# Modulation sums of a two-block transformer kernel: column quarters of the array, a ScalarE copy and a transpose in place of matmuls with one moving column

## The reference

```
ml = ada_mods(c, ada_w[i], ada_b[i])          # six vectors of 1024 from c:  c @ ada_w[i] + ada_b[i], c through silu
mc = ada_mods(c_ctx, ada_w[i], ada_b[i])      # the same for the context, where it is still needed
hl = modulate(rms_norm_2(x, norm1_g[i]), ml[0], ml[1])
x  = x + ml[2] * yl
x  = x + ml[5] * sq_relu_mlp(modulate(rms_norm_2(x, norm2_g[i]), ml[3], ml[4]), mlp_w1[i], mlp_w2[i])
```

## Time and profile before

| what | value |
|---|---|
| median of 3 runs | 3950.78 us (3943.45 to 3952.15) |
| span of the profiled execution | 3942.7 us |
| profiled execution's own time | not listed apart from the span; the nearest of the three runs took 3943.45 us |
| TensorE busy (matmuls) | 3801.9 us, 96% of the span |
| TensorE weight loads (beside matmuls) | 2605.5 us, 66% |
| VectorE, ScalarE, GpSimd busy | 50%, 24%, 15% |
| DMA | 87 GB/s on the mean |
| granted TensorE clock, mean | 0.981 of full |

### The profile page before, as it was taken

The page is one execution under the profiler, slowest core; times in us unless marked ns, Lnnn a source line. Parts: engine busy times, 40 slices in busy tenths (PEclk is TensorE's granted clock), DMA queues, the critical chain, the costliest instruction groups (busy, mean ns, idle before and its releaser), DMA issues.

```text
span 3942.7 us, 42262 instructions
## 1 busy us (share of the span) xinstructions
PE 3801.9 (96%) x16296; PEld 2605.5 (66%) x16296; DVE 1982.2 (50%) x3455; ACT 956.5 (24%) x2193; POOL 585.3 (15%) x476
## 2 busy tenths in 40 slices
PE   9999999999999999999999899999999999999997
PEld 4458446545655566555554578888568888778886
DVE  2654345635673566555300845654765566244343
ACT  1142214621452212112201632021312111212020
POOL 1001000001000111111200511112432111111111
PEclk8999999999999999999999999999999999999999
DMA  3112331022002123323112414443202444112221
GB/s 130 64 44 87 99 106 56 1 76 86 25 1 63 65 90 124 120 94 128 54 64 76 80 44 150 171 167 101 75 22 86 170 172 150 70 64 86 86 86 43
DMA packets 226949, 342.46 MB, mean 87 GB/s; under 512 B 32256, under 2 KB 100512, under 8 KB 226720
## 3 DMA queue, kind: packets, MB, share of 16 engines
q1 hardware_dynamic: 201552, 321.65, 23.8%
q0 software_dynamic: 6816, 10.01, 1.3%
q10 hardware_dynamic: 18384, 8.11, 0.8%
HBM read 334.08 MB, written 4.06 MB: 86 GB/s over the span
## 4 chain that ended last, share of the span: by engine, by line
PE 90%; DVE 4%; ACT 2%; issue 1%; POOL 1%; DMA 0%; ACTq 0%; DVEq 0%; POOLq 0%
PE psum L1743 44%; PE psum L1493 30%; PE psum L1861 3%; PE psum L1808 3%; PE psum L1838 2%; PE psum L1599 1%; PE psum L1453 1%; DVE small L2735 1%; ACT arena L2192 1%; POOL arena L2916 1%; PE psum L1551 1%; PE psum L1522 1%; PE psum L1534 1%; ACT arena L2180 0%; PE psum L1820 0%
## 5 line engine op out<-in xcount | busy, mean ns | idle before, releaser
L1493 PE MATMUL psum<-HC,ring 128*128 128x256 f32 (+1 forms) x3152 | 1023.7, 484 | 14.2 <-ACT HC L2111 4.5
L1493 PEld LDWEIGHTS psum<-HC,ring 128*128 128x128 f32 x3152 | 599.2, 192 | 430.3 <-issue 371.6
L1743 PE MATMUL psum<-arena,ring 128*128 128x256 f32 (+1 forms) x2304 | 600.4, 416 | 5.2 <-ACT arena L1975 5.2
L1743 PEld LDWEIGHTS psum<-arena,ring 128*128 128x128 f32 x2304 | 435.5, 190 | 147.6 <-ACT arena L1975 10.0
L1743 PE MATMUL psum<-arena 128*128 128x256 f32 (+1 forms) x1792 | 472.3, 417 | 0.4
L1743 PE MATMUL psum<-HC,ring 128*128 128x256 f32 (+1 forms) x1792 | 438.5, 399 | 10.9 <-ACT arena L1975 4.7
L1743 PEld LDWEIGHTS psum<-arena 128*128 128x128 f32 x1792 | 340.4, 190 | 115.4 <-ACT arena L1980 0.7
L1743 PEld LDWEIGHTS psum<-HC,ring 128*128 128x128 f32 x1792 | 341.6, 192 | 86.7 <-issue 10.9
L2873 POOL TENSOR_TENSOR ring<-ring 128x1024 f32<-128x1024 f32 (+1 forms) x80 | 217.4, 2717 | 1220.8 <-DVE arena L2260 1199.4
L2425 DVE SCALAR_TENSOR_TENSOR arena<-ring,cond,arena 128x512 f32<-128x512 f32 x448 | 319.6, 750 | 8.0
L2329 DVE TENSOR_TENSOR arena<-psum,arena 128x384 f32<-128x384 f32 (+2 forms) x80 | 44.5, 556 | 382.6 <-PE psum L1743 382.6
(11 more groups left out here) (229 smaller groups left out, 3907.6 us busy)
## 6 DMA issues: line engine op xcount, KB each, us to landing
ring<-in_mlp_w SPq DMA_DIRECT2D x64, 2048.0 KB, 8.9
ring<-in_ada_w SPq DMA_DIRECT2D x48, 2048.0 KB, 7.9
ring<-in_na_qkv SPq DMA_DIRECT2D x6, 2048.0 KB, 7.9
ring<-in_ab_in SPq DMA_DIRECT2D x5, 2048.0 KB, 8.8
ring<-in_cd_in SPq DMA_DIRECT2D x4, 2048.0 KB, 9.8
ring<-in_pw SPq DMA_DIRECT2D x8, 1024.0 KB, 6.7
ring<-in_at_qkv SPq DMA_DIRECT2D x3, 2048.0 KB, 8.0
ring<-in_ab_out SPq DMA_DIRECT2D x2, 2048.0 KB, 7.7
```

The lines of the kernel that those rows point to most:

```text
L1493: last = nc.tensor.matmul(out, lhs, rhs, start=(k == 0), stop=(k == len(t.pairs) - 1))
L1743: last = nc.tensor.matmul(bank(at, u["T"], u["T"] * m), w[:, i, P * m:P * m + P], x[:, i, :], start=(opens and m == 0 and i == 0), stop=(i ...
```

## The change

Each vector's partial sums are now reduced over the partitions in the other direction. The four pieces are the moving operand, and the weights are 32 equal columns of `mean_d`; piece m goes to the column quarter 32 m to 32 m + 31 of the array, and its sums come out as 32 equal rows in PSUM, divided by 1024. ScalarE copies bank 7 (128 x 128 per vector) back to SBUF, over the first 128 columns of `partial`. One transpose per vector then turns this, so that column 32 m holds the 128 sums of piece m. VectorE multiplies by D, adds the bias and writes `mods` as before, in one instruction that replaces one.

The single place on TensorE becomes two. `modulation_rows` (wait for `ada_summed`, the row matmuls) stands before the last tile of the next group, or, in a fast stage, after the fourth product of the next unit. The transposes stand where the old matmuls stood, at the end of the group or unit, behind a new wait for ScalarE's copy (`ada_rows`). ScalarE has its copy at the same two places.

```diff
+        def ada_sums(v):
+            return bank(7, P, P * v)
+        def ada_rows_of(v):
+            return partial[:, v, 0:P]
...
@@ TensorE @@
-            def modulation(a):
-                layer, j = a[1], a[2]
+            def modulation_rows():
+                if not pending:
+                    return
+                vs = ada_vectors(*pending[0][1:])
                 pe.wait_ge(ada_summed, n["ada"] + 1)
                 open_bank(7)
-                vs = ada_vectors(layer, j)
                 for v in range(vs):
                     for m in range(4):
-                        last = nc.tensor.matmul(bank(7)[:, 2 * m + v:2 * m + v + 1], partial[:, v, P * m:P * m + P],
-                                                ones[:, :], start=(v == 0 and m == 0), stop=(v == vs - 1 and m == 3),
+                        last = nc.tensor.matmul(ada_sums(v)[32 * m:32 * m + 32], mean_d[:, 0:32],
+                                                partial[:, v, P * m:P * m + P], start=(v == 0), stop=(v == vs - 1),
                                                 skip_group_check=True)
                 last.then_inc(ada_ready, 1)
-                n["ada"] += 1
-                bank_freed[7] = (ada_taken, n["ada"])
+                bank_freed[7] = (ada_rows, n["ada"] + 1)
             def ride(a):
                 if pending:
-                    modulation(pending.pop())
+                    vs = ada_vectors(*pending.pop()[1:])
+                    n["ada"] += 1
+                    pe.wait_ge(ada_rows, n["ada"])
+                    open_bank(7)
+                    for v in range(vs):
+                        last = nc.tensor.transpose(ada_sums(v), ada_rows_of(v), ident[:, :])
+                    last.then_inc(ada_turned, 1)
+                    bank_freed[7] = (ada_taken, n["ada"])
...
                     for t in tiles:
+                        if t is tiles[-1]:
+                            modulation_rows()
...
                         for kind, job, of in u["after"].get(p, []):
                             side[kind](job, of)
+                        if p == u["order"][3]:
+                            modulation_rows()
@@ ScalarE @@
+            def copy_rows():
+                if not pending:
+                    return
+                n["ada"] += 1
+                vs = ada_vectors(*pending.pop()[1:])
+                act.wait_ge(ada_ready, n["ada"])
+                nc.scalar.activation(partial[:, 0:vs, 0:P], bank(7, vs * P).rearrange("p (v f) -> p v f", v=vs),
+                                     ACT.Copy).then_inc(ada_rows, 1)
...
+                        if t is tiles[-1]:
+                            copy_rows()
+                            pending.extend(to_ride)
...
+                        if p == u["order"][3]:
+                            copy_rows()
+                            pending.extend([u["a"]] if u["a"] else [])
@@ VectorE @@
-                    dve.wait_ge(ada_ready, n["ada"] + 1)
+                    dve.wait_ge(ada_turned, n["ada"] + 1)
                     bias = V(f"ada_b{layer}")[:, 4 * j:4 * j + 4].unsqueeze(2).to_broadcast([P, 4, vs])
-                    nc.vector.tensor_tensor(mods[:, layer % 2, 4 * j:4 * j + 4, 0:vs],
-                                            bank(7)[:, 0:8].rearrange("p (m v) -> p m v", v=2)[:, :, 0:vs], bias,
-                                            ALU.add).then_inc(ada_taken, 1)
+                    sums = bank(7, vs * P).rearrange("p (v m r) -> p m v r", v=vs, m=4)[:, :, :, 0]
+                    nc.vector.scalar_tensor_tensor(mods[:, layer % 2, 4 * j:4 * j + 4, 0:vs], sums, float(D), bias, ALU.mult,
+                                                   ALU.add).then_inc(ada_taken, 1)
```

More of the change, by code:

```diff
@@ L321, in build_program @@
         ada_summed, ada_ready, ada_taken = sem("ada_summed"), sem("ada_ready"), sem("ada_taken")
+        ada_rows, ada_turned = sem("ada_rows"), sem("ada_turned")
         squares_ready, mean_ready, sd_ready = sem("squares_ready"), sem("mean_ready"), sem("sd_ready")
@@ L1896, in _ @@
             n = dict(tile=0, sq=0, mean=0, unit=0, read=0, scaled=0, idx=0, misc_pe=0, misc_act=0, norm=0, pv=0, normed=0,
-                     ctx=0, conv=0)
+                     ctx=0, conv=0, ada=0)
             hid_base = [0]
@@ L1911, in preload @@
                 step(nc.scalar.activation(unused[:, :], eps, function))
+            pending = []
+            def copy_rows():
[6 more added lines that the diff above has]
+                                     ACT.Copy).then_inc(ada_rows, 1)
             def project(st):
@@ L1916, in project @@
                 for b, tiles, a in st["groups"]:
+                    if a:
+                        to_ride = [a]
+                    else:
+                        to_ride = []
                     for t in tiles:
                         n["tile"] += 1
+                        if t is tiles[-1]:
+                            copy_rows()
+                            pending.extend(to_ride)
                         if t.taker != "act":
```

## The result

The changed kernel takes 3962.09 us (median of 6 runs, 3956.5 to 3970.75) against 3944.32 us (6 runs, 3942.88 to 3952.15) for the kernel before on the same chips. The ratio is 1.0045, 95% interval 1.0034 to 1.0055: slower by 17.8 us, where 23.2 was forecast.

A forecast was written before the change was run, and what follows sets the result against it. TensorE, busy 3801.9 of 3942.7 us, was taken to bound the kernel. Terms -14.2 (work), +29.4 (waits) and +8 (clock) sum to +23.2 us on 3950.8, giving 3974.0 us, range 3956 to 3994.

The forecast's parts named there:

- the sign: Whole kernel: slower by 23.2 us, as new waits and clock drops outweigh the gain on TensorE; slower had chance 0.82.
- The wait moved up: TensorE before the row matmuls: waits for VectorE's partial sums, three products or one tile earlier, 29.4 us in all.
- the quarters: Row matmuls on TensorE: all four column quarters stream at once, 0.21 us per vector; one-vector visit about 0.55 us.
- rivals 1 and 2: Row matmuls: quarters overlap only in pairs (13.7 us more, chance 0.15) or not at all (41 us more, chance 0.05).
- rival 2: Row matmuls: the quarters don't overlap, 41 us more, 4015 us; chance 0.05.
- the transposes: End of each ride on TensorE: two records per transpose at about 0.11 us each, 0.22 us per vector.
- The gain on TensorE: Modulation rides: old matmuls at 59.2 us replaced by rows and transposes at 45.0 us, 14.2 us saved.
- Nothing queued ahead of it on ScalarE waits for anything later than TensorE's rows: ScalarE's new copy: hidden, 0.47 us for 256 columns, needed three products or a tile later; no cost in the sum.
- the clock: TensorE after the longer new waits: drops to half the granted clock, 8 us, ends 0 and 16.
- Rival 3: New waits before the rows: absorbed by later slack, kernel faster, 3937 us with none left; chance of faster 0.07.
- Rival 4: New waits half absorbed, 14 to 20 us, no clock drop: +0 to +6 us, not measurable; chance 0.11.
- the range: Whole kernel's time: 3956 to 3994 us, said to leave out rival 2, Rival 3 and half of Rival 4.

The follow-up runs named there:

- e1_rows_late: The changed kernel with row matmuls and ScalarE's copy in fast stages moved from behind the fourth product to behind the sixth: 3940.01 us, ratio 0.9983.
- e2, e7b: A follow-up kernel; the text given does not say which of the described runs carries this label, so its change and time can't be assigned.
- e3a: Label not spelled out; apparently the changed kernel with four more row matmuls per vector, each to its own column quarter: 3980.63 us, ratio 1.0092.
- e3b: Label not spelled out; apparently the changed kernel with four more row matmuls per vector, all to the first column quarter: 4011.45 us, ratio 1.0168.
- e6_rows_mid_tile: The changed kernel with rows behind the sixth product in fast stages and in the middle of the last tile in project stages: 3938.8 us, ratio 0.9986.

## Why the prediction was right

**Right: the sign and its cause.** The wait moved up by three products or a tile was forecast at 29.4 us from the overhang of the partial sums, and the trace has 29.7, with the large single waits as listed: 5.79 twice (5.90 forecast), 3.44 (3.45), 1.58 twice (1.69). In layers 2 and 3 the single waits are off by more (in one place 1.56 for 0.72, in another none for 0.50), and the sum is nearer than they are. (The last unit of the MLP in layers 2 and 3 goes in an order of its own, 1, 6, 2, 7, 4, 5, 3, which the description of the kernel leaves out; there too three products follow the fourth.) That nothing gives it back was shown by the kernel with the wait alone.

**Right: the quarters.** 0.55 us for the visit of a one-vector ride was forecast and measured, and rivals 1 and 2 are refuted by the doubled rows: 0.21 us for eight added records on four quarters, 0.85 on one. The Trainium skill ("TensorE: Matmul & The Clock Gate", Part 3, The mechanism) lets a weight load overlap with running matmuls only when the row group differs. The trace disagrees: the four quarters share their rows, and the eight weight loads of the ride at 1610.96, 0.106 to 0.109 us each, lie within 0.16 us, beside the row matmuls that start there too. That sentence speaks of weight loads only, so rival 2, by which the quarters' matmuls would run one by one, took more from it than it says.

**Mis-sized: the transposes.** "Four records take 0.66 us", and from that "0.22 us per vector", took two records for one transpose. It is one: 64 records for 64 transposes, 0.11 us each. The gain on TensorE is 20.8 us, not 14.2. The four records that I read the earlier trace rows were four transposes of 128 columns, not two: the loop in `turn` makes one per block of 128, and the kernel with ordinary matmuls shows the two records of those.

**Missed: the squares.** "Nothing queued ahead of it on ScalarE waits for anything later than TensorE's rows" was true, but the question was what is queued behind the copy. Seven squares were, in two places, and GpSimd and TensorE behind them: 6.0 us that the sum had at nothing. The timeline before shows that ScalarE's squares run far ahead of the norm; the prediction argued from the engine's busy share and from what stands ahead of the copy.

**Wrong: the clock.** I put 8 us on it. Half-clock stretches do follow the three longest waits (a granted clock of 0.55 over the 3.4 us after the one at 1412), and they cost what a row shows, 3.66 us for a product of 2.58. But others that the kernel before has, near 439, 507, 589 and 681, are gone, and the table's row is -0.4 us, the clock loss alone -0.3. Which of them fall away because of the change, no run shows. The two errors above nearly cancel (-6.6 and +6.0), which is luck; with 0.3 on the waits and 8.4 on the clock they are the 8.7 us between the two sums of the table; the medians differ by 3.3 more than the spans, so that +17.8 was measured for +23.2. The other 6.5 us between 3974.0 and 3962.1 are the base: the kernel before had a median of 3944.3 on these chips, and 3950.8 in the runs I forecast from.

Rival 3, the absorbed wait, isn't borne out: in layers 2 and 3 one wait is missing where 0.50 was forecast (near 3157 in the changed kernel), but the one ahead of it was longer than forecast, 1.56 for 0.72, and the sum of these layers is 5.1 us for 4.2. Rival 4 and the range don't fit together in the prediction: 3956 is 5.2 us above the base, so the range leaves out nearly all of a rival from +0 to +6, and not half. The result at +17.8 isn't touched by it.

## What to carry to other kernels

When an instruction is moved up on its engine, what its input's producer is doing at that moment counts, not whether it is done in the end; the overhang can be read from the trace before, place by place, and it was right to 0.3 us of 29 in the sum, to 0.1 us for the longest waits and to 0.8 us for the worst of the short ones. A new wait on an engine that is a quarter busy is free only if nothing that another engine needs is queued behind it. A reduction over partitions for a few vectors is cheaper on four column quarters than with one moving column, as soon as the copy and the turn back have a product's time to hide in: here 0.66 against 0.90 us for one vector and 0.98 against 1.79 for two, and with the waits mended the whole kernel is 0.56% faster than before.

## What was not expected of the hardware

A float32 transpose of 128 x 128 is one record and takes 0.11 us, while the same product as an ordinary matmul is two records and 0.22 us. Four column quarters stream at the full rate of one each: eight records in the time of two, 0.21 us. And stretches at half clock come and go between kernels in places that no edit touches: between 703 and 755 it is 20 us in one kernel (e1_rows_late), 14 to 17 us in four others (e2, e3a, e3b, e7b), 3 us in e6_rows_mid_tile, none in the change, the kernel before and the other three. The loss by clock in a profiled run, half the busy time at 0.50, lies between 54 and 73 us over the eleven traces, a spread as large as the effect studied. What decides where they fall stays open.
